# A recurrence's first three projection tiles moved among another's last samples, and the masks moved behind the loads

## The reference

```
z  = rms_norm(x) @ w_in                      # 2048 x 18640 columns
zs, za, qb, kb, vb, glo, zb, ga, gb = split(z)
xs = zs + (prev(zs) - zs) * mu               # token shift; prev of a sample's first token: its state row
r, k, v, w_lo, a_lo = split(xs)              # RWKV-7 branch: 32 heads of 64
S  = S * w + (S @ a) b^T + v k^T;  y = S @ r
oa = (layer_norm(y) + sum(r*k*r_k) * v) * silu(za)
ob = rms_norm(chunked_gla(qb, kb, vb, g(glo))) * silu(zb)   # GLA branch: 4 heads, 256 x 512 states
out = x + rms_norm((sigmoid(ga) * oa + sigmoid(gb) * ob) @ w_out)
```

## Time and profile before

| | us |
|---|---|
| median of 3 runs | 3428.09 |
| the three runs | 3411.41, 3429.99, 3428.09 |
| the profiled execution | 3422.14 |
| its span, first to last instruction | 3420.6 |
| TensorE's mean granted clock, share of full speed | 0.961 |

### The profile page before, as it was taken

How to read it: one execution, slowest core, us unless ns; L and a number is a source line. 1 busy time by engine, 2 the same in 40 slices (tenths; PEclk the granted TensorE clock), 3 DMA queues, 4 the chain that set the end, 5 groups by cost and what they waited for, 6 DMA issues and landing times. The chain is left out here.

```text
span 3420.6 us, 78091 instructions
## 1 busy us (share of the span) xinstructions
PE 3187.0 (93%) x33143; PEld 2929.2 (86%) x33143; DVE 1720.2 (50%) x2451; ACT 1057.7 (31%) x1688; POOL 395.0 (12%) x804
## 2 busy tenths in 40 slices
PE   3799999999985999999999999999999999995896
PEld 2698797897964999999999999999999999994895
DVE  3244554444642564564664564565565565563224
ACT  3233332422411332332332343243243243242222
POOL 2100101001002120120120121011021021011000
PEclk9899999999986999999999999999999999997998
DMA  3222433324313222222222221231122122122332
GB/s 90 67 76 61 145 87 117 114 62 136 94 60 104 59 65 54 62 65 54 62 65 55 61 77 46 58 77 51 53 77 59 45 77 64 40 64 102 97 86 92
DMA packets 368530, 255.07 MB, mean 75 GB/s; under 512 B 19412, under 2 KB 347600, under 8 KB 366288
## 3 DMA queue, kind: packets, MB, share of 16 engines
q1 hardware_dynamic: 342592, 184.18, 19.8%
q0 software_dynamic: 25600, 66.02, 6.1%
HBM read 212.69 MB, written 37.45 MB: 73 GB/s over the span
## 5 line engine op out<-in xcount | busy, mean ns | idle before, releaser
L365 PE MATMUL psum<-act_hi,w_hi 128*128 128x280 f32 (+3 forms) x5216 | 1602.6, 307 | 78.1 <-DVE w_lo L351 39.3
L367 PE MATMUL psum<-act_hi,w_lo 128*128 128x280 f32 (+3 forms) x5216 | 1531.9, 294 | 0.0
L366 PE MATMUL psum<-act_lo,w_hi 128*128 128x280 f32 (+3 forms) x5216 | 1530.3, 293 | 0.0
L365 PEld LDWEIGHTS psum<-act_hi,w_hi 128*128 128x128 f32 (+2 forms) x5216 | 990.2, 190 | 152.5 <-issue 111.1
L366 PEld LDWEIGHTS psum<-act_lo,w_hi 128*128 128x128 f32 (+2 forms) x5216 | 990.1, 190 | 5.4 <-issue 0.7
L367 PEld LDWEIGHTS psum<-act_hi,w_lo 128*128 128x128 f32 (+2 forms) x5216 | 989.8, 190 | 1.1
L351 DVE TENSOR_TENSOR w_lo<-raw,w_hi 128x1024 fp32r<-128x1024 f32 (+1 forms) x326 | 396.5, 1216 | 306.2 <-ACT w_hi L343 294.0
L343 ACT CAST w_hi<-raw 128x1024 fp32r<-128x1024 f32 (+1 forms) x326 | 339.6, 1042 | 80.9 <-DMA raw<-in_w_in_dram 38.9
L1987 PE MATMUL psum<-arena 64*64 64x64 f32 x9216 | 309.8, 219 | 1.1 <-issue 0.2
L1987 PEld LDWEIGHTS psum<-arena 64*64 64x64 f32 x9216 | 285.8, 134 | 27.1 <-issue 27.1
L1544 POOL DMA_DIRECT2D out_s_rwkv_dram<-arena x128 | 77.6, 614 | 1538.0 <-ACT arena L1690 1538.0
(11 more groups left out here) (327 smaller groups left out, 3472.3 us busy)
## 6 DMA issues: line engine op xcount, KB each, us to landing
raw<-in_w_in_dram SPq DMA_DIRECT2D x288, 512.0 KB, 4.5
arena<-in_state_gla_dram POOLq DMA_DIRECT2D x32, 512.0 KB, 5.2
out_s_gla_dram<-arena POOLq DMA_DIRECT2D x32, 512.0 KB, 3.3
raw<-in_w_out_dram SPq DMA_DIRECT2D x32, 512.0 KB, 4.3
ob_dram<-arena POOLq DMA_DIRECT2D x16, 280.0 KB, 2.9
arena<-ob_dram POOLq DMA_DIRECT2D x16, 280.0 KB, 5.0
m_dram<-arena POOLq DMA_DIRECT2D x16, 280.0 KB, 2.6
arena<-m_dram SPq DMA_DIRECT2D x4, 1120.0 KB, 12.1
```

Source lines behind the costliest of these rows:

```text
L365: pe.matmul(out, hi, act_hi[:, k, cols], start=(k == 0), stop=False)
L366: pe.matmul(out, hi, act_lo[:, k, cols], start=False, stop=False)
L367: mm = pe.matmul(out, lo, act_hi[:, k, cols], start=False, stop=(k == KT - 1))
```

## The change

Stage C's head: GpSimd issues the load of gk_w first and makes the masks after it. ScalarE and TensorE wait for the masks only behind the four first tiles, VectorE behind its third split. gate_logits stands between the halves of tile 0; ScalarE splits tile 1 and evacuates tile 0's first half earlier.

Stage C's last head: the projection of stage D (pd) is set up in stage C, its buffers z_ lie where k_g was, and tiles 0 to 2 of turn 0 follow tile 11, at the places where the other heads have tiles 12 to 14. Tiles 0 and 1 are evacuated into z_ there, tile 2 stays in the banks.

The semaphores of stage C are cleared by four engines, each a fourth.

Stage D's head: loads begin with tile 3; GpSimd does the small loads and the first two seeds ahead of the masks, and the two saves and the third seed behind them. TensorE makes tile 3 whole in turn 0 between the two head sums and waits for the masks ahead of the state transposes. Later turns keep their order. The functions seed, open_turn and load_lora only move.

```diff
-        def to_shift_buffer(eng, i, mine, proj, t, z, n=P):
-
-            proj.evacuated.count = 2 * t
-            eng.wait_ge(proj.half.sem, proj.half.at(i, 2 * t + 1))
-            nc.scalar.copy(z[0:n, 1:1 + HALF], bank[0][0:n, 0:HALF]).then_inc(proj.evacuated.sem, 1)
-            eng.wait_ge(proj.evacuated.sem, proj.evacuated.next(i))
+        def to_shift_buffer(eng, i, mine, proj, t, z, n=P, halves=(0, 1)):
+
+            proj.evacuated.count = 2 * t + halves[0]
+            if 0 in halves:
+                eng.wait_ge(proj.half.sem, proj.half.at(i, 2 * t + 1))
+                nc.scalar.copy(z[0:n, 1:1 + HALF], bank[0][0:n, 0:HALF]).then_inc(proj.evacuated.sem, 1)
+                eng.wait_ge(proj.evacuated.sem, proj.evacuated.next(i))
+            if 1 not in halves:
+                return
...
+                sp.wait_ge(pc.lo.sem, pc.lo.at(LAST_HEAD, 24))
+                sp.sem_inc(pd.lo.sem, 2)
+                for t in range(3):
+                    load_rwkv(sp, 0, t)
...
+                def load_gate(at):
+                    pool.dma_start(gk_w[LORA:LORA + GLORA, :], gla_gk_w2[0, :, at]).then_inc(load_gk.sem, 16)
+                load_gate(slice(0, BK_))
                 mine, i = masks, 0
                 pool.memset(level_mask, 0.0).then_inc(mine.sem, 1)
...
-                act.wait_ge(masks.sem, masks.count)
                 pc.split_hi(act, i, mine, 0)
+                pc.split_hi(act, i, mine, 1)
                 gate_bias(i, mine, 0, 0)
                 gate_bias(i, mine, 0, 1)
-                pc.split_hi(act, i, mine, 1)
+                evacuate(i, 0, 0)
                 gate_logs(i, mine, 0)
-                for t in range(4):
+                evacuate(i, 0, 1)
+                for t in range(1, 4):
                     evacuate(i, t, 0)
-                    if t:
-                        pc.split_hi(act, i, mine, t + 1)
+                    pc.split_hi(act, i, mine, t + 1)
                     evacuate(i, t, 1)
+                act.wait_ge(masks.sem, masks.count)
...
-                    more = (lambda t: None) if last else (lambda t: pc.split_hi(act, i, mine, t))
+                    
+                    def more(t):
+                        if not last:
+                            pc.split_hi(act, i, mine, t)
+                        elif t < 15:
+                            pd.split_hi(act, 0, mine, t - 12)
+
+                    def next_tile(t, half):
+                        if not last:
+                            evacuate(i, t, half)
+                        elif t < 14:
+                            to_shift_buffer(act, 0, mine, pd, t - 12, z_[t - 12], halves=(half,))
+
...
+                    if last:
+                        act.sem_inc(pd.half.sem, 1)
                     more(12)
...
+                    if last:
+                        act.sem_inc(pd.half.sem, 2)
                     more(13)
...
-                    if not last:
-                        evacuate(i, 12, 0)
+                    next_tile(12, 0)
...
+                    next_tile(12, 1)
+                    more(14)
+                    next_tile(13, 0)
+                    next_tile(13, 1)
+                    more(15)
+                    next_tile(14, 0)
...
-                dve.wait_ge(masks.sem, masks.count)
                 pc.split_lo(dve, i, mine, 0)
+                pc.split_lo(dve, i, mine, 1)
                 for n in range(2):
                     gate_abs(i, 0, n)
-                pc.split_lo(dve, i, mine, 1)
+                pc.split_lo(dve, i, mine, 2)
+                dve.wait_ge(masks.sem, masks.count)
                 for n in range(2):
                     gate_scan(i, mine, 0, n)
-                for t in range(2, 5):
+                for t in range(3, 5):
                     pc.split_lo(dve, i, mine, t)
...
-                pe.wait_ge(masks.sem, masks.count)
...
-                gate_logits(0, 0, 0)
                 fill = pc.steps(pe, 0, 0)
                 for _ in range(16):
                     next(fill)
+                gate_logits(0, 0, 0)
                 gate_logits(0, 0, 1)
                 for _ in fill:
                     pass
                 for t in range(1, 4):
                     pc.whole(pe, 0, t)
+                pe.wait_ge(masks.sem, masks.count)
+
+                def rwkv_tiles():
+                    steps = chain(*(pd.steps(pe, 0, t) for t in range(3)))
+                    for half in range(2):
+                        pe.wait_ge(pc.evacuated.sem, pc.evacuated.at(LAST_HEAD, 23 + half))
+                        pe.sem_inc(pd.evacuated.sem, 1)
+                        for _ in range(KT):
+                            next(steps)
+                            yield
+                    yield from steps
 
...
-                    fill = chain(*(pc.steps(pe, i, t) for t in range(4, 12 if last else 16)))
+                    fill = chain(*(pc.steps(pe, i, t) for t in range(4, 12 if last else 16)), rwkv_tiles() if last else ())
...
-                for s in own_signals:
+                for s in own_signals[0::4]:
                     pool.sem_clear(s.sem)
+
+            @block.scalar
+            def _(act):
+                for s in own_signals[1::4]:
+                    act.sem_clear(s.sem)
...
-                    pd.load(sp, i, t, lambda h: w_in[0, h * D // 2:(h + 1) * D // 2, ds(i * P + col, P)])
-                for t in range(3):
-                    load(0, t)
                 for i in range(NPAIR):
                     for t in range(3, 6 if i == LAST_TURN else 9):
-                        load(i, t)
+                        load_rwkv(sp, i, t)
...
+                load_lora(slice(0, P))
+                pool.sem_inc(stored.sem, 1)
+                mine, i = g_first, 0
+                for t in range(2):
+                    pool.memset(z_[t][:, 0:1], 0.0).then_inc(mine.sem, 1)
+                    pool.wait_ge(mine.sem, mine.next(i))
+                    seed(pool, i, mine, t)
+                mine = masks
                 pool.memset(causal, 1.0).then_inc(mine.sem, 1)
...
-                for tile in (a_r[:, NF, :], b_k[:, NF, :], v_pad, a8, z_[0][:, 0:1], z_[1][:, 0:1]):
+                for tile in (a_r[:, NF, :], b_k[:, NF, :], v_pad, a8):
...
+                mine = g_first
                 open_turn(i, mine, 0)
...
-                mine, i = s_first, 0
-                pd.split_hi(act, i, mine, 0)
-                pd.split_hi(act, i, mine, 1)
-                evacuate(act, i, mine, 0)
-                pd.split_hi(act, i, mine, 2)
-                evacuate(act, i, mine, 1)
...
-                mine, i = v_order, 0
-                for t in range(3):
-                    pd.split_lo(dve, i, mine, t)
+                i = 0
...
-                pe.wait_ge(masks.sem, masks.count)
-                pe.sem_inc(pd.evacuated.sem, 2)
-                pd.whole(pe, 0, 0)
-                pd.whole(pe, 0, 1)
...
-                    fill = pd.steps(pe, i, 2)
-                    for _ in range(12):
+                    fill = chain(*(pd.steps(pe, i, t) for t in (2, 3)[i == 0:]))
+                    for _ in range(12 if i else 0):
                         next(fill)
                     pe.wait_ge(k_squared.sem, k_squared.at(i, 1))
                     pe.sem_inc(waited.sem, 1)
                     head_sums(sq, 6, square_sum)
-                    for _ in fill:
-                        pass
-                    fill = pd.steps(pe, i, 3)
-                    for _ in range(20):
-                        next(fill)
+                    for _ in range(40):
+                        next(fill, None)
                     pe.wait_ge(rk_ready.sem, rk_ready.at(i, 1))
                     pe.sem_inc(waited.sem, 1)
                     head_sums(sq, 2, rk_sum)
                     for _ in fill:
                         pass
 
+                    if i == 0:
+                        pe.wait_ge(masks.sem, masks.count)
+                        pe.sem_inc(waited.sem, 1)
```

More of the change, by code:

```diff
@@ L514, in build, with load_rwkv @@
         pc = Projection("c", 12)
+        pd = Projection("d", 6)
+        z_ = [arena[:, n * ZW:(n + 1) * ZW] for n in range(2)]
+        assert 2 * ZW <= o_first
+        TILES = (D, 0, 2 * D, COL_ZA, COL_GA, COL_GB)
+        def load_rwkv(sp, i, t):
+            col = TILES[t % 6] + t // 6 * P
+            pd.load(sp, i, t, lambda h: w_in[0, h * D // 2:(h + 1) * D // 2, ds(i * P + col, P)])
         v_order, s_order, g_order = own("c_vector", DCV), own("c_scalar", DCS), own("c_pool", DCG)
@@ L988, in merge, with more @@
                         dve.wait_ge(signal.sem, signal.next(i))
-                    more = (lambda t: None) if last else (lambda t: pc.split_lo(dve, i, mine, t))
+                    def more(t):
+                        if not last:
+                            pc.split_lo(dve, i, mine, t)
+                        elif t < 15:
+                            pd.split_lo(dve, 0, mine, t - 12)
                     diff(1)
@@ L1290, in _ @@
             def _(pool):
```

(45 more changed lines are left out.)

25 lines of the change are left out of this document (removed).

## The result

The changed kernel took 3377.43 us, the median of 4 runs (3372.64 to 3383.47), beside 3425.26 for the kernel before in the same place (4 runs, 3411.41 to 3429.99): a ratio of 0.9868, 95% interval 0.9834 to 0.9902. A second set of 5 runs gave 0.9868 again (0.9849 to 0.9887). The forecast was 3376. The profiled execution took 3374.94, its span 3373.4, 47.2 shorter than before.

What follows compares the result with a forecast made beforehand. TensorE, busy nine tenths nearly everywhere, was taken as the bound, so only its holes could pay. From the profiled 3422.14, -14.4 + 4.9 - 3.0 - 33.5 = -46.0 gave 3376 us, range 3358 to 3396.

Steps and rivals of the forecast that it cites:

- Part 1: Head of stage C: without mask waits TensorE starts 8.1 after the first load, at 125.2; gain 14.4, ends 12.5 to 15.5.
- The rival that something else held TensorE until 134.7: Head of stage C: a load or a bank still holds TensorE, so no gain there; 3390 us, chance 0.12.
- Part 2: Last head of stage C: 96 steps, 37 us, put among the samples cost only 4.9, range 3 to 6.2.
- head 2's row: Samples with tiles among them took 57.0 in head 2, 50.8 in the last head: the basis for the tiles' price.
- The rival of 37 us: Last head's samples: the tiles are not hidden and cost their own 37 in place of 4.9; 3408 us, chance 0.07.
- That of samples stretched by their states: Last head: state store and load lose their overlap, eight samples lose 63 us more; over 3439 us, chance 0.02.
- Part 3: Seam between stages C and D: 48 clears shared by four engines save 3.0 us, range 0 to 3.2.
- two bounds: Seam: the clears' gain lies between 0 and 3.2, at most three quarters of a 4.3 difference between seams.
- Part 4: Head of stage D: gram products read 41.5 after the stage's start in place of 75.06; gain 33.5, ends 37.9 and 19.5.
- unblocked term: Head of stage D: GpSimd's third seed done 16.7 after the start if VectorE blocks nothing.
- The blocked one: Head of stage D: third seed at 20.4 with as much blocking by VectorE as before; 21.0 was taken.
- the first rival: Head of stage D: masks starve while VectorE's chain runs, tile 2 leaves the banks at 35; 3390 us, chance 0.12.

Runs made afterwards that it cites:

- stage C's head alone: Kernel before with only the edits of stage C's head (gate-weight load ahead of masks, waits for masks behind the first tiles): ratio 0.9962 to before over 9 runs.
- put back: Changed kernel with stage C's head as it was before, masks first and waits at the start: median 3385.46 us, ratio 0.9909 to before.
- the last two of the table: Changed kernel, third seed ahead of stage D's masks, turn 0's tile 3 made earlier: ratio 0.9871; same plus turn 0's state loads ahead of masks: 3362.75 us, 0.9838.
- thin tiles: Changed kernel with only the first of three products made for the three tiles among the last head's samples: 3375.89 us in one run.
- masks first: Changed kernel with GpSimd's old order in stage D, masks ahead of small loads, seeds and saves: 3384.41 us in one run.
- third seed first: Changed kernel with stage D's two saves, third seed and four small memsets ahead of its masks, run twice: ratios 0.9866 and 0.9849 to before.

## Why the prediction was right

| part | predicted | measured |
|---|---|---|
| 1, head of stage C | -14.4 | -13.6 (alone -14.0, put back +13.2) |
| 2, three tiles among samples | +4.9 | +5.3 |
| 3, clears | -3.0 | -1.9 |
| 4, head of stage D | -33.5 | -32.6 |
| sum | -46.0 | -42.9 |

The profile's difference, 47.2, has 4.3 more, none of it foreseen: stage B's end came 0.9 earlier, the heads took 3.55 longer, the stretch from copy-out to stores 0.1 less, and all behind the first gram read 6.85 less. Of the 6.85, 1.65 lie between the gram read and turn 1's bonus. The two kernels with the old stage D take 122.6 and 122.8 there, the changed kernel 121.1 twice, and the others 119.3 to 121.2, the last two of the table aside (turn 1 less gram); so these may be the change's own, but no run tests it. The heads, but for one split by ScalarE in the last, and turns 1 to 15 are the same code in all twelve profiles. Heads took 802.7 to 816.9; from turn 1's bonus to turn 15's it was 1781.3 in the kernel before and 1768.4 in the kernel with stage C's head alone, whose stage D is the same. So the median came within 1.4 of 3376 in part by luck: stretches that the prediction did not speak of, chance of the execution for the most part, made up for 3 us of over-estimated parts. (The ends of the four parts add up to -53.6, not -53.4; this moves no bound by more than 0.2.)

*Part 1* held in mechanism. TensorE began 124.50 - 116.12 = 8.4 after SyncE's first load, 8.1 expected. The rival that something else held TensorE until 134.7 falls with its first matmul, at 124.50.

*Part 2*'s estimate by head 2's row was right to 0.4. Whose time the price is it did not say; the thin tiles show that it is TensorE's. The rival of 37 us falls with 5.3, though TensorE is indeed full now, and by the estimate above half of the hiding goes with the clock. That of samples stretched by their states falls with the updates (L976, now L1008): from the first sample's to the last's 41.04, after 40.00 before and 40.83 in head 2. The other 4.2 lie ahead of the first update and behind the last, about half each.

*Part 3* was sized near the upper of two bounds. The clears themselves gave 2.45 of the 3.0; the stage's first instruction took back 0.5.

*Part 4*'s weighing between 16.7 and 20.4 for the third seed was the right step. The unblocked term holds: with the masks first the seed ends 17.7 after the stage's start, and 1.0 of that are two small copies behind the masks that ran beside VectorE's shift and took 0.66 and 0.72 in place of 0.20. The blocked one was low, 22.1 in place of 21.0: the masks alone lost 5.2 to VectorE, where 4.3 had been allowed for everything. The rest of the chain, from tile 2's evacuation to the gram read, took 20.1 (1080.01 to 1100.15) for 20.5. The Trainium skill, page "SBUF — State Buffer", section "SBUF: two separate sides", says that VectorE and GpSimd hold their shared port pair for a whole instruction. The trace agrees, 13.15 alone and 18.36 beside the chain; but starved, as the rule taken to its end would have it, GpSimd was not, and the first rival's 35 for tile 2 didn't come: ScalarE began to evacuate it at 22.3.

## What to carry to other kernels

When a wait is taken off a head of a stage, follow the released engine until it stops again and name what it stops for: here masks, then VectorE's chain, then loads that had been queued behind the masks, then the masks again. Each was found by one bracket in a timeline, or by its absence. A work item that one engine does for nobody in particular (masks) still delays whatever stands behind it in that engine's queue, small copies and load issues too; put those ahead. Judge a gain of 6 us in 3400 by the distance between two marks, not by the whole time.

## What the hardware showed that I had not expected

The granted clock fell to one half for a stretch at the end of heads, and its length differs between executions of the same code. Windows of the kernel before, the changed kernel, and the second run of the kernel with the third seed first (columns as above):

```profile
835.50:838.90 3.40, 3.40 (x15) 3.32 (x15) 0.00 (x0) 0.00 (x0) 0.00 (x0) 0.50 0.03 5
```
```profile
821.10:831.30 10.20, 10.20 (x37) 8.21 (x36) 0.00 (x0) 0.10 (x1) 0.00 (x0) 0.50 0.01 2
```
```profile
825.00:845.50 20.50, 20.50 (x78) 18.08 (x78) 0.00 (x0) 1.06 (x3) 0.00 (x0) 0.50 0.00 1
```

At 0.50, 1.2 of 2.4 GHz, 15, 37 and 78 matmuls went through; a full tile's 96 take 12.32, so they would have taken 1.9, 4.7 and 10.0, and 1.5, 5.5 and 10.5 us were lost. TensorE was busy throughout these stretches; just ahead of them, at full clock, it had been busy for 4.24 of 5.50, 3.84 of 5.10 and 3.75 of 5.00.

There are more of them than these three. In the kernel before TensorE stood at 0.50 for some 10.2 us between 180 and 990, in the changed kernel for 20.5, in its second profile for 17.1. With stage C's head alone it was 20.4, 10.2 of it from about 600, where the kernel before has 3.4, and 3.4 at about 402, where it has none. Over the twelve profiles the heads' length rises with this sum: 802.7 at 10.2 and 13.6 us, 809 at 24 to 27, 816.9 at 41.0. So the 3.55 of the changed kernel and the 2.7 of stage C's head alone go with the clock. Why one stretch is longer than another no run here shows.
